# Two of the four weight forms of the first gate/up round are summed by accumulating DMAs on GpSimd's queue in place of VectorE

## The reference

```python
x = x + rms_norm(mix, g_mix_post[layer])
h = rms_norm(x, g_ffn_pre[layer])
ff = (jax.nn.silu(h @ w_gate[layer]) * (h @ w_up[layer])) @ w_down[layer]
x = x + rms_norm(ff, g_ffn_post[layer])
```

## Time and profile before

| | us |
|---|---|
| median of 3 runs | 1922.96 (1921.97 to 1924.96) |
| the profiled execution's own time | 1920.78 |
| its span, first to last instruction | 1918.9 |
| PE busy in the span | 1881.9 (98%) |
| DVE busy | 1515.7 (79%) |
| ACT busy | 915.4 (48%) |
| POOL busy | 53.4 (3%) |

### The profile page before, as it was taken

One profiled execution on the slowest core, in us unless ns is written; L12 is line 12 of the kernel. 1 busy time (PEld: TensorE's weight loads), 2 busy tenths in 40 slices (PEclk: granted clock), 3 DMA queues, 4 the chain that ended last, 5 costly groups with the idle time before them and its releaser, 6 DMA issues.

```text
span 1918.9 us, 22133 instructions
## 1 busy us (share of the span) xinstructions
PE 1881.9 (98%) x8730; PEld 1559.5 (81%) x8730; DVE 1515.7 (79%) x1606; ACT 915.4 (48%) x1220; POOL 53.4 (3%) x41
## 2 busy tenths in 40 slices
PE   8999999999999999999999999999999999999998
PEld 6888788888887778888888888888888788888886
DVE  5763496676466988888988888888889888888888
ACT  6331394455464645454554545545455733333332
POOL 1210040000000000000000000000000000000000
PEclk9999999999999999999999999999999999999999
DMA  8434201116675245263462643725436866547563
GB/s 245 115 95 114 87 24 61 61 67 246 237 263 197 80 141 183 92 230 113 140 218 78 209 136 117 248 83 175 163 107 230 307 251 236 205 163 268 212 228 131
DMA packets 205251, 314.28 MB, mean 164 GB/s; under 512 B 7555, under 2 KB 142812, under 8 KB 199260
## 3 DMA queue, kind: packets, MB, share of 16 engines
q1 hardware_dynamic: 202112, 306.21, 46.5%
q10 hardware_dynamic: 3036, 6.66, 1.1%
HBM read 263.01 MB, written 52.98 MB: 165 GB/s over the span
## 4 chain that ended last, share of the span: by engine, by line
PE 61%; DVE 3%; issue 1%; DMA 1%; ACT 0%; DVEq 0%; ACTq 0%
PE pair L2584 13%; PE pair L2586 13%; PE pair L2585 13%; PE pair L2633 6%; PE pair L2635 6%; PE pair L2634 6%; PE pair L2595 1%; PE pair L2654 1%; PE pair L2653 1%; PE pair L2652 1%; DVE unit_lo L1866 1%; DMA w_b<-in_w_down 1%; DVE ring_lo L2111 0%; DVE xf_lo L1860 0%; DVE w2a L1891 0%
## 5 line engine op out<-in xcount | busy, mean ns | idle before, releaser
L2584 PE MATMUL pair<-unit_hi,xf_hi 128*128 128x512 f32 x1224 | 481.7, 394 | 7.9 <-DVE unit_lo L1866 7.9
L2586 PE MATMUL pair<-unit_hi,xf_lo 128*128 128x512 f32 x1224 | 477.0, 390 | 0.0
L2585 PE MATMUL pair<-unit_lo,xf_hi 128*128 128x512 f32 x1224 | 476.4, 389 | 0.0
L2584 PEld LDWEIGHTS pair<-unit_hi,xf_hi 128*128 128x128 f32 x1224 | 229.8, 188 | 58.3 <-issue 7.3
L2586 PEld LDWEIGHTS pair<-unit_hi,xf_lo 128*128 128x128 f32 x1224 | 229.7, 188 | 48.6
L2585 PEld LDWEIGHTS pair<-unit_lo,xf_hi 128*128 128x128 f32 x1224 | 230.0, 188 | 46.3
L459 DVE TENSOR_TENSOR wlo<-raw,whi 128x2048 fp32r<-128x2048 f32 (+2 forms) x62 | 131.0, 2119 | 94.5 <-ACT whi L452 94.4
L2633 PE MATMUL pair<-ring_hi,hfs 128*128 128x512 f32 x480 | 187.4, 390 | 1.4 <-ACT ht L1314 0.8
L452 ACT ACTIVATE whi<-raw 128x2048 fp32r<-128x2048 f32 (+2 forms) x62 | 109.6, 1775 | 163.8 <-PE pair L712 155.9
L2634 PE MATMUL pair<-ring_lo,hfs 128*128 128x512 f32 x480 | 186.8, 389 | 0.0
L2635 PE MATMUL pair<-ring_hi,hfs 128*128 128x512 f32 x480 | 186.8, 389 | 0.0
(11 more groups left out here) (377 smaller groups left out, 3407.1 us busy)
## 6 DMA issues: line engine op xcount, KB each, us to landing
w_b<-in_w_down SPq DMA_DIRECT2D x40, 1024.0 KB, 5.1
h_forms<-h_stage SPq DMA_DIRECT2D x71, 512.0 KB, 4.9
raw<-in_w_o SPq DMA_DIRECT2D x32, 1024.0 KB, 5.1
hfs<-h_forms SPq DMA_DIRECT2D x30, 1024.0 KB, 8.3
raw<-in_w_in SPq DMA_DIRECT2D x18, 1024.0 KB, 5.8
w1a<-in_w_gate SPq DMA_DIRECT2D x16, 512.0 KB, 3.6
w1a<-in_w_up SPq DMA_DIRECT2D x16, 512.0 KB, 5.4
w1b<-in_w_gate SPq DMA_DIRECT2D x16, 512.0 KB, 3.7
```

The costliest lines, as they stand in the source:

```text
L2584: nc.tensor.matmul(dst, a[0], w[0], start=(at, k) == (0, 0), stop=False)
L2585: nc.tensor.matmul(dst, a[0], w[1], start=False, stop=False)
L2586: last = nc.tensor.matmul(dst, a[1], w[0], start=False, stop=(at, k) == (3, 1))
```

## The change

In round 0 VectorE no longer makes T3 and T4. T2 is stored with its sign turned, as T2' = T1 - b22 (the same instruction with its operands exchanged). GpSimd's queue then issues ten transfers that add to what lies at their destination (`accum_op`):

- T3: for each half one transfer from slot to slot, w2 added to w0. It gives b11 + T2', which is -T3.
- T4: for each half four transfers from DRAM, b21 added to w2. It gives T2' + b21, which is T4. The four are the two weights by two pairs of row blocks, 128 x 2 x 256 elements each, in runs of 1 KB.

So products 2 and 3 come out with the other sign, and the three `c_sum` of round 0 that take them subtract. SP no longer loads the second b21 (four transfers of 512 KB), and before it loads the next round's b12 it no longer waits for T4's sum. ScalarE's copies for T3's and T4's units wait for `t3_in` and `t4_in`, on which the transfers count. Rounds 1 to 10 are as before; `sums_before(b)` corrects their counts of `g_sum`.

```diff
+            def add_t2_to_b11(half):
+                s1, s2, _ = slots(0)
+                pool.wait_ge(u_lo, unit_no(0, 0, 2 * half + 1) + 1)
+                pool.wait_ge(g_sum, half + 3)
+                nc.gpsimd.dma_start(w_slot[s1][half][:, :, :], w_slot[s2][half][:, :, :],
+                                    accum_op=ALU.add).then_inc(t3_in[half], 16)
+            def add_b21_to_t2(half):
+                place = w_slot[slots(0)[1]][half]
+                pool.wait_ge(u_lo, unit_no(0, 2, 2 * half + 1) + 1)
+                pool.wait_ge(t3_in[half], 16)
+                for w_v, c0 in ((wg_v, 0), (wu_v, 256)):
+                    for k in (0, 2):
+                        nc.gpsimd.dma_start(place[:, k:k + 2, c0:c0 + 256],
+                                            w_v[:, 1, 4 * half + k:4 * half + k + 2, 0:256],
+                                            accum_op=ALU.add).then_inc(t4_in[half], 16)
+            for half in range(2):
+                add_t2_to_b11(half)
+            for half in range(2):
+                add_b21_to_t2(half)
...
                             if f_ == 3:
-                                load(b, "b21", v // 2)
+                                if b:
+                                    load(b, "b21", v // 2)
...
                                 if f_ == (5 if b else 6):
-                                    sp_.wait_ge(g_sum, 8 * b + 7 + v // 2)
+                                    if b:
+                                        sp_.wait_ge(g_sum, sums_before(b) + 7 + v // 2)
...
                 elif f_ in (2, 3, 6):
-                    act.wait_ge(g_sum, 8 * b + {2: 2, 3: 4, 6: 6}[f_] + v // 2 + 1)
+                    if b == 0 and f_ != 2:
+                        act.wait_ge((t3_in if f_ == 3 else t4_in)[v // 2], 16 if f_ == 3 else 64)
+                    else:
+                        act.wait_ge(g_sum, sums_before(b) + {2: 2, 3: 4, 6: 6}[f_] + v // 2 + 1)
...
-                    nc.vector.tensor_tensor(s2, s3, t1, ALU.subtract).then_inc(g_sum, 1)
+                    a, c = (s3, t1) if b else (t1, s3)
+                    nc.vector.tensor_tensor(s2, a, c, ALU.subtract).then_inc(g_sum, 1)
...
-                nc.vector.tensor_tensor(dst, a, product_bank(b, f_)[:, :, :], ALU.add).then_inc(c_added, 1)
+                turned = b == 0 and f_ in (2, 3)
+                nc.vector.tensor_tensor(dst, a, product_bank(b, f_)[:, :, :],
+                                        ALU.subtract if turned else ALU.add).then_inc(c_added, 1)
...
             first_units(3, 1, 2)
-            weight_sum(0, 3, 0)
             first_units(3, 2, 3)
             x_form_lo(3, 0)
             first_units(3, 3, 4)
-            weight_sum(0, 3, 1)
             first_units(4, 0, 1)
...
             c_sum(0, 3)
-            weight_sum(0, 6, 0)
             first_units(5, 3, 4)
-            weight_sum(0, 6, 1)
             first_units(6, 0, 2)
```

More of the change, by code:

```diff
@@ L317, in build @@
         g_sum = sem("g_sum")
+        t3_in = [sem(f"t3_in{i}") for i in range(2)]
+        t4_in = [sem(f"t4_in{i}") for i in range(2)]
         u_hi = sem("u_hi")
@@ L644, in unit_place, with sums_before @@
             return unit_hi[u % 3], unit_lo[u % 3]
+        def sums_before(b):
+            return 8 * b - 4 if b else 0
         def t1_count(b, half):
-            return (2, 1)[half] if b == 0 else 8 * b + half + 1
+            return (2, 1)[half] if b == 0 else sums_before(b) + half + 1
         def product_bank(b, f_):
@@ L668, in build @@
             s1_, s2_, s3_ = slots(b_)
-            for what_, slot_ in ((("b11", s1_), ("b21 first", s3_), ("b12", s2_), ("b22", s3_), ("b21", s1_)) if b_ == 0
+            for what_, slot_ in ((("b11", s1_), ("b21 first", s3_), ("b12", s2_), ("b22", s3_)) if b_ == 0
                                  else (("b11", s1_), ("b12", s2_), ("b22", s3_), ("b21", s1_))):
@@ L1414, in form_hi @@
                     act.wait_ge(u_lo, 28 * ROUNDS - 4)
-                    act.wait_ge(g_sum, 8 * ROUNDS)
+                    act.wait_ge(g_sum, sums_before(ROUNDS))
                 elif n == 14:
@@ L1881, in weight_sum @@
                         dve.wait_ge(used, Q_FFN)
-                    nc.vector.tensor_tensor(s2, s3, t1, ALU.subtract).then_inc(g_sum, 1)
+                    a, c = (s3, t1) if b else (t1, s3)
+                    nc.vector.tensor_tensor(s2, a, c, ALU.subtract).then_inc(g_sum, 1)
                 elif form == 3:
-                    dve.wait_ge(g_sum, 8 * b + half + 3)
+                    dve.wait_ge(g_sum, sums_before(b) + half + 3)
                     dve.wait_ge(u_lo, unit_no(b, 0, 2 * half + 1) + 1)
@@ L1888, in weight_sum @@
                     dve.wait_ge(*loaded(b, "b21", half))
-                    dve.wait_ge(g_sum, 8 * b + half + 5)
+                    dve.wait_ge(g_sum, sums_before(b) + half + 5)
                     dve.wait_ge(u_lo, unit_no(b, 2, 2 * half + 1) + 1)
```

## The result

The changed kernel takes 1929.62 us (median of 7 runs, 1927.04 to 1931.61) against 1923.18 us (median of 7, 1921.97 to 1924.96): ratio 1.003, 95% interval 1.002 to 1.004. It is slower by 6.4 us, where 4.6 us of gain were forecast.

A forecast was written before the change was run, and what follows sets the result against it. In round 0 VectorE sets the pace and TensorE waits; elsewhere TensorE is busy. Removing the waits gives -4.6 us, the rest 0: 1922.96 - 4.6 = 1918.4 us (-0.24%), range 1917 to 1929, the forecast's own 1917.5 to 1919.8.

The forecast's parts named there:

- What bounds the kernel, and the gain: Round 0: VectorE sets the pace and TensorE waits; removing four VectorE sums was to give back 4.6 us.
- the upper bound: Most that round 0 could gain: unit 26 starting at 687.4 instead of 692.60, so 5.2 us.
- the order of time on VectorE: VectorE in round 0 would end unit 23's work at 678.4, before TensorE wants it at 678.9.
- Unit 24's want: Time at which TensorE, without waits in round 0, would want unit 24: 681.7, giving T4's first half the limit 679.3.
- D: Time of an accumulating transfer for 1 MB, one half of T3 or T4: taken as 9.2 us, two passes.
- the landing times of T4: T4's two halves in round 0 would land at 666.3 and 675.5, in time by 3.8 us or more.
- the limit of 685.0: Latest landing of T4's second half that keeps TensorE, which wants unit 26 at 687.4, from waiting.
- slow adding: Rival: with D = 13.8 T4's second half lands at 693.9, net +4.3, so 1927.3 us; chance 0.14.
- slow issuing: Rival: T4's eight transfers in GpSimd's queue issue too slowly; 1926.8 us at 5 us each; chance 0.16, 0.09 of it slower.
- g: Time of each T4 issue on GpSimd's queue; had to be under 4.0 us, no change at 4.5.
- issues of 4 us or more on GpSimd's queue: Sign in the trace that would show the forecast wrong.
- the clock is no part of this case: Granted clock in round 0 is full (1.00), so the prediction gave it no share in the time.

The follow-up runs named there:

- e1_slot: Changed kernel, but T4 added from slot to slot by one transfer per half (runs of 8 KB), SP loading the second b21 again: 1920.87 us, ratio 0.9989.
- e2_runs2k: Changed kernel, but T4's eight 256 KB transfers from DRAM have 128 runs of 2 KB, so T4's values differ: 1916.66 us (one run).
- e1_t3_only: Changed kernel, but only T3 by transfers; VectorE adds T4 from the second b21, which SP loads again: 1919.77 us, ratio 0.9983.
- e2_mix: Changed kernel, but T4's first half by one slot-to-slot transfer, its second half summed on VectorE behind unit 24's rest: 1918.22 us, ratio 0.9974.
- e2_slot_pieces: e1_slot with each half of T4 in four slot-to-slot transfers of 256 runs of 1 KB: 1942.48 us (one run).
- e1_pieces128: Changed kernel with T4's eight transfers of 256 runs made sixteen of 128 runs (128 KB each): 1930.49 us, ratio 1.0037.

## Why the prediction was wrong

**What bounds the kernel, and the gain: right.** VectorE's chain held TensorE up in round 0, and what was taken off it came back as time. From unit 12 to the transposes before unit 26 the changed kernel takes 688.84 - 650.64 = 38.2 us, where it was 692.25 - 648.98 = 43.3: 5.1 us gained, 4.6 forecast, 5.2 the upper bound. Also right was the order of time on VectorE: unit 23's rest was forecast to end 29.4 us after unit 12's start (678.4 - 649.0) and ended 29.7 after it (680.3 - 650.6). The subtracting sums and the loads that SP no longer makes cost nothing that the trace shows. (Unit 24's want comes to 681.6, where the prediction has 681.7; nothing hangs on it.)

**The time of T3's transfers: right.** D was taken as 9.2 us; 8.8 and 7.2 were measured, and both halves were there before ScalarE asked. That is 1.9 and 1.6 times a load's 4.6, so the rule quoted from the Trainium skill ("Collectives: The Full Stack", The bandwidth ceiling), half the rate of a copy, agrees roughly with this trace for runs of 8 KB.

**The step that failed** is the landing times of T4: "With 9.2 they land at 647.9, 657.1, 666.3 and 675.5, all in time by 3.8 us or more". It priced a half of T4 as one megabyte, D, though the diff shows that it is four transfers of 256 runs each. Where the sum had 9.2 us for each, a half of T4 took 20.0 us (653.12 to 673.1) and 22.2 us (673.37 to 695.6). So the last landing came 44.9 us after unit 12's start, at 693.9 in the forecast's times instead of 675.5, and 8.9 us past the limit of 685.0. The price of such a transfer goes by its runs: in the mean 5.4 us for 256 adding runs of 1 KB, 2.8 for 128 of 1 KB and 2.7 for 128 of 2 KB. The prediction named the short runs under slow adding, as a reason, and gave them no price; it named the eight issues as a rival, slow issuing, with g = 5 us giving 1926.8, and gave that 0.16. That rival comes nearest: issues of 4 us or more on GpSimd's queue, the sign that the prediction named, came with 5.4 in the mean. But the time was not that of making an issue; it depends on the runs and on adding, which the prediction had put under the other rival.

Two smaller things were missing. Four loads for round 1 wait for unit 25's `lo`, and VectorE, now freer, let them start earlier: at 683.68, 33.0 us after unit 12's start, where it was 687.69, 38.7 after. So they met T4's seventh transfer, which landed after 7.3 us where the others took 4.2 to 5.7. By my estimate that is some 2.6 us of the delay (7.3 less 4.7, the mean of the other seven). And "the clock is no part of this case" held for the kernel before alone: no rival counted what a long wait takes from the clock, 1.5 us here.

**What the loss is made of.** In the trace, unit 26 starts 8.9 us later than it could (698.07 against 688.84 + 0.35); its first seven matmuls cost 0.2 us more each, 1.5 us. Less 5.1 gained, that is +5.3; the stretch shows +5.2. The medians differ by 6.4. The other 1.2 us may lie within what the executions of one kernel differ by, and I can't say where they are: in the profiled execution of the changed kernel 1.7 us come before unit 2 (its start is at 615.75 instead of 614.05), but e1_slot and e2_runs2k don't have them (613.91 and 613.87), while e1_t3_only and e2_mix have most of them (615.35 and 615.70) and are fast all the same.

**Which cause, then.** The runs rule out DRAM as the source (e2_slot_pieces), the bytes (e2_runs2k) and the number of transfers (e1_pieces128). What is left is the number of runs, or, what these runs can't tell from it, of packets: 272 adding packets in 5.4 us, 144 in 2.7 to 2.8, 80 copying ones in 2.2. VectorE's instructions are not needed for it: the last transfer ran from its issue at 690.65 to its landing in 4.9 us, all of it while VectorE did nothing (684.4 to 696.70), as long as those beside a busy VectorE. The inference of the Trainium skill ("SBUF — State Buffer", Who interferes with whom) was that making descriptors is spared by such instructions, and nothing here speaks against it.

Open is what inside the queue makes it wait. Room for a bounded number of packets in flight would explain why T4's transfers were issued one landing apart and why three small ones went back to back in e1_pieces128. But no single number fits all the bursts: in that run, at 674.8 only one transfer of 144 packets was in flight, and the next was still issued only at 678.11, after it had landed. Work that GpSimd does behind the issue would fit the total as well.

## What to carry to other kernels

Price a transfer by its contiguous runs, not by its bytes alone: the same megabyte, added from slot to slot, took 8.2 us in 128 runs and 23.5 in 1024, and with an adding transfer on GpSimd's queue the difference is exposed, since the transfers behind it wait. Where work is moved off an engine that holds up TensorE for 5 us, move as much as closes the gap and no more: with three of the four sums moved and the last one placed a few instructions later on VectorE, the whole gain was there (1918.2 us); moving that last one too gave 1929.6 in short runs and 1920.9 in long ones (e1_slot). And ask what the relieved engine will start earlier: here it was loads that met the new transfers.

## What the runs showed of the hardware

After an idle time of 8.63 us TensorE's matmuls started 0.43 us apart until 701.13 instead of 0.23, and the granted clock of that stretch (the number before the last two) was 0.52, against 1.00 behind it:

```profile
698.07:701.13 3.06, 3.06 (x8) 2.44 (x8) 3.06 (x3) 2.68 (x6) 0.00 (x0) 0.52 0.00 0
701.13:704.00 2.87, 2.87 (x14) 2.36 (x13) 2.82 (x3) 1.06 (x1) 0.00 (x0) 1.00 0.94 298
```

That is the lower of the clock's two levels (1.2 of 2.4 GHz). After 11.31 us idle in e1_pieces128 it was 0.50 from 699.10 to 703.08. After 1.74 us idle in e1_slot the next matmuls came at the usual 0.23, at a clock of 1.00. So a wait of some 9 us cost 1.5 us more than its length here.

An accumulating transfer slowed plain loads beside it more than its bytes suggest. In e1_slot, adding 1 MB from slot to slot took 8.2 us, and in that time the loads moved 0.32 MB; a load alone moves its 1 MB in 4.6 us. The same load took 6.6 us in e2_slot_pieces, where the adding was cut into short runs. The load of b21 in e1_slot ended at 677.4 (666.38 + 11.0), 4.0 us after the adding transfer; the last part of it ran beside the next load.
